# Latent attention: how the rotated queries of head pairs two to four are made and multiplied

## The reference, cut to what matters

```python
q = rms_norm(h @ w_dq) @ w_uq         # 8 heads x (128 plain + 64 rotary columns)
k_rope = rope(h @ w_kr)               # 64 rotary columns, one set for all heads
k_plain, v = split(rms_norm(h @ w_dkv) @ w_ukv)
q = concat(q_plain, rope(q_rope))     # rope: x * cos + swap_halves(x) * (-sin, sin)
s = (q @ concat(k_plain, k_rope).T) / sqrt(192)   # causal, then softmax, then @ v
```

## Time and profile before

| | us |
|---|---|
| median of 3 runs | 1338.31 (1337.6 to 1339.15) |
| the profiled execution's own time | 1336.54 |
| its span in the trace, first to last instruction | 1334.8 |
| PE busy in the span | 1306.4 |
| DVE (VectorE) busy | 754.4 |
| ACT (ScalarE) busy | 524.6 |

### The profile page before, as it was taken

The page is one execution under the profiler, slowest core; times in us unless marked ns, Lnnn a source line. Parts: engine busy times, 40 slices in busy tenths (PEclk is TensorE's granted clock), DMA queues, the critical chain, the costliest instruction groups (busy, mean ns, idle before and its releaser), DMA issues.

```text
span 1334.8 us, 16283 instructions
## 1 busy us (share of the span) xinstructions
PE 1306.4 (98%) x6203; PEld 1080.2 (81%) x6203; DVE 754.4 (57%) x1041; ACT 524.6 (39%) x739; POOL 32.8 (2%) x31
## 2 busy tenths in 40 slices
PE   8999999999999999999999999999999999989997
PEld 7788888888888777788888888888888878878876
DVE  6854544444448675654444544554767578875554
ACT  6443223233334554433223223334233355665334
POOL 0510000000000000000000000000000000010000
PEclk9999999999999999999999999999999999999999
DMA  5343232223242201233222222233543121112211
GB/s 188 95 126 94 94 94 94 79 87 103 90 111 65 57 33 64 79 97 108 94 94 94 94 79 87 88 105 100 158 125 128 32 63 48 48 64 96 95 63 64
DMA packets 120888, 119.43 MB, mean 89 GB/s; under 512 B 13500, under 2 KB 117896, under 8 KB 120584
## 3 DMA queue, kind: packets, MB, share of 16 engines
q1 hardware_dynamic: 120784, 118.76, 28.3%
q10 hardware_dynamic: 56, 0.01, 0.0%
HBM read 114.57 MB, written 4.19 MB: 89 GB/s over the span
## 4 chain that ended last, share of the span: by engine, by line
PE 90%; DVE 5%; ACT 2%; issue 1%; DMA 0%; DVEq 0%; SPq 0%; ACTq 0%
PE psum L1807 27%; PE psum L1809 26%; PE psum L1808 26%; PE psum L1991 1%; PE psum L2014 1%; PE psum L2176 1%; PE psum L2148 1%; PE psum L2162 1%; PE psum L2302 1%; ACT w_hi L647 1%; PE psum L2001 1%; DVE w_lo L1121 1%; PE psum L2256 1%; PE psum L1845 1%; PE psum L1825 0%
## 5 line engine op out<-in xcount | busy, mean ns | idle before, releaser
L1807 PE MATMUL psum<-xg_hi,w_hi 128*128 128x512 f32 x1088 | 432.2, 397 | 1.4 <-DVE emb L1701 0.9
L1809 PE MATMUL psum<-xg_hi,w_lo 128*128 128x512 f32 x1088 | 424.0, 390 | 0.0
L1808 PE MATMUL psum<-xg_lo,w_hi 128*128 128x512 f32 x1088 | 423.8, 389 | 0.0
L1807 PEld LDWEIGHTS psum<-xg_hi,w_hi 128*128 128x128 f32 x1088 | 204.6, 188 | 44.6 <-issue 1.5
L1809 PEld LDWEIGHTS psum<-xg_hi,w_lo 128*128 128x128 f32 x1088 | 204.3, 188 | 43.4
L1808 PEld LDWEIGHTS psum<-xg_lo,w_hi 128*128 128x128 f32 x1088 | 204.6, 188 | 40.4 <-issue 1.2
L1255 DVE TENSOR_TENSOR w_lo<-w_raw,w_hi 128x2048 fp32r<-128x2048 f32 x40 | 91.8, 2295 | 145.6 <-ACT w_hi L740 145.6
L1282 DVE TENSOR_TENSOR w_lo<-w_raw,w_hi 128x2048 fp32r<-128x2048 f32 x32 | 73.4, 2293 | 115.6 <-ACT w_hi L766 115.6
L1807 PE MATMUL psum<-act_hi,w_hi 128*128 128x512 f32 x352 | 137.2, 390 | 0.0
L1808 PE MATMUL psum<-act_lo,w_hi 128*128 128x512 f32 x352 | 137.0, 389 | 0.0
L1809 PE MATMUL psum<-act_hi,w_lo 128*128 128x512 f32 x352 | 136.9, 389 | 0.0
(11 more groups left out here) (355 smaller groups left out, 1614.7 us busy)
## 6 DMA issues: line engine op xcount, KB each, us to landing
w_raw<-in_ffn_w_gate SPq DMA_DIRECT2D x22, 1024.0 KB, 5.1
w_raw<-in_ffn_w_up SPq DMA_DIRECT2D x22, 1024.0 KB, 5.1
w_raw<-in_w_in SPq DMA_DIRECT2D x16, 1024.0 KB, 5.4
w_raw<-in_ffn_w_down SPq DMA_DIRECT2D x16, 768.0 KB, 4.8
w_raw<-in_ffn_w_down SPq DMA_DIRECT2D x16, 640.0 KB, 4.5
w_raw<-in_mla_w_o SPq DMA_DIRECT2D x4, 1024.0 KB, 5.2
w_raw<-in_w_out SPq DMA_DIRECT2D x4, 1024.0 KB, 5.0
w_raw<-in_w_ple_gate SPq DMA_DIRECT2D x4, 1024.0 KB, 4.9
```

The lines of the kernel that those rows point to most:

```text
L1807: pe.matmul(o, wh, xh, start=start, stop=False, skip_group_check=True)
L1808: pe.matmul(o, wh, xl, start=False, stop=False, skip_group_check=True)
L1809: return pe.matmul(o, wl, xh, start=False, stop=stop, skip_group_check=True)
```

## The change

For pairs two to four (pr = 1 to 3) VectorE rotates the queries itself. It multiplies all 128 rows of `u` by cos into `squares[:, 0]` (one instruction), multiplies 32-row quarters by sin into the swapped places of `squares[:, 1]` (four instructions, `rope_swap`, two for each head), and subtracts (one instruction, `rope_sum`). ScalarE rounds each head's 64 rows into half of an fp32r tile (two instructions), and VectorE writes the residue into the other half (two, `rope_lo`). The tiles are free ones of `xg_hi`. The keys' rotated 64 rows are written once as `kr_st`: rounded part twice, on both halves, and residue twice, on both halves (two ScalarE and two VectorE instructions). The rotary score is then two fp32r passes over 128 partitions, the stacked query against the rounded keys and against their residue. Pair one keeps `q_rope` and the fp32 product. `q_rope` has one buffer instead of two.

The order of VectorE for a pair whose `u` is recorded in step s0 (s0 = 4, 12, 20): iteration s0 + 1: cos, first swap, normalise, second swap. Iteration s0 + 2: after the row maximum, `rope_sum`. Iteration s0 + 3: after the residue of `kn0` and after normalising, `rope_lo`. ScalarE's two roundings stand first in its iteration s0 + 3, before the rounding of `kn0`. The bank of `u` is free only after the second swap, and the scores of step s0 + 4 wait for `rope_lo`.

```diff
-        q_rope = sb("q_rope", [P, 2, 2, T], stack=mla_mem)
+        q_rope = sb("q_rope", [P, 2, T], stack=mla_mem)
+        kr_st = sb("kr_st", [P, 2, T], F32R, mla_mem)
...
         def proj_released(x):
+            if x[1] == "u":
+                return sem("rope_turned"), 8 * x[0] + (1 if x[0] else 4)
             return (sem("values_kept"), VALUED.index(x) + 1) if x in VALUED else (sem("proj_ready"), RESIDUED.index(x) + 1)
+        def rope_step(s, later):
+            return [pr for pr in range(1, HEADS // 2) if later < s <= NB * HEADS and (pr, "u") in after_step(*divmod(s - 1 - later, NB))]
+        def rope_tiles(pr, e):
+            x = xg_hi[:, QR + 2 * (pr % 2) + e, :]
+            return (x[64 * e:64 * e + 64, :], x[64 - 64 * e:128 - 64 * e, :], x)
...
@@ ScalarE, for s in range(NB * HEADS + 3): @@
+                    for pr in rope_step(s, 2):
+                        act.wait_ge(sem("rope_turned"), 8 * pr + 2)
+                        act.activation(rope_tiles(pr, 0)[0], squares[0:64, 0, :], ACT.Copy)
+                        act.activation(rope_tiles(pr, 1)[0], squares[64:128, 0, :], ACT.Copy).then_inc(*mark(f"rope_hi{pr}"))
...
+                    if s == 3:
+                        act.activation(kr_st[0:64, 0, :], kr[0:64, :], ACT.Copy)
+                        act.activation(kr_st[64:128, 0, :], kr[0:64, :], ACT.Copy).then_inc(*mark("kr_st"))
...
@@ VectorE @@
+                def rope_swap(pr, e):
+                    ps = proj_result(PROJ_ORDER.index((pr, "u")))
+                    for r0, r1 in ((64 * e, 64 * e + 32), (64 * e + 32, 64 * e)):
+                        dve.tensor_tensor(squares[r0:r0 + 32, 1, :], ps[r1:r1 + 32, :], sin_t[r1:r1 + 32, :], ALU.mult).then_inc(sem("rope_turned"), 1)
+                def rope_sum(pr):
+                    dve.wait_ge(sem("rope_turned"), 8 * pr + 1)
+                    dve.tensor_tensor(squares[:, 0, :], squares[:, 0, :], squares[:, 1, :], ALU.subtract).then_inc(sem("rope_turned"), 1)
+                def rope_lo(pr):
+                    dve.wait_ge(*at(f"rope_hi{pr}"))
+                    for e in range(2):
+                        hi, lo, _ = rope_tiles(pr, e)
+                        dve.tensor_tensor(lo, squares[64 * e:64 * e + 64, 0, :], hi.bitcast(F32), ALU.subtract).then_inc(sem("rope_turned"), 1)
...
                     if what == "u":
...
+                        if pr:
+                            dve.tensor_tensor(squares[:, 0, :], ps[:, :], cos_t[:, :], ALU.mult).then_inc(sem("rope_turned"), 1)
+                            rope_swap(pr, 0)
+                            return
...
@@ VectorE, for s in range(NB * HEADS + 1): @@
                         row_max(s)
+                    for pr in rope_step(s, 1):
+                        rope_sum(pr)
                     if s:
                         for t in after_step(*divmod(s - 1, NB)):
                             proj(*t)
                     if s:
                         normalise(s - 1)
+                    for pr in rope_step(s, 0):
+                        rope_swap(pr, 1)
+                    for pr in rope_step(s, 2):
+                        rope_lo(pr)
+                    if s == 4:
+                        dve.wait_ge(*at("kr_st"))
+                        for r in range(0, P, 64):
+                            low = dve.tensor_tensor(kr_st[r:r + 64, 1, :], kr[0:64, :], kr_st[0:64, 0, :].bitcast(F32), ALU.subtract)
+                        low.then_inc(*mark("kr_lo"))
...
@@ TensorE, scores(s) @@
-                    pe.wait_ge(sem("proj_ready"), proj_count(h // 2, f"kn{h % 2}", f"qn{h % 2}", "u"))
-                    pe.wait_ge(sem("rope_turned"), 3 * (h // 2) + 3)
+                    pe.wait_ge(sem("proj_ready"), proj_count(h // 2, f"kn{h % 2}", f"qn{h % 2}"))
+                    pe.wait_ge(sem("rope_turned"), 8 * (h // 2) + 4)
+                    if s == 2 * NB:
+                        pe.wait_ge(*at("kr_lo"))
...
-                    pe.matmul(o, q_rope[:, h // 2 % 2, hs, q], kr[:, k], start=False, stop=False, skip_group_check=True)
+                    if h < 2:
+                        pe.matmul(o, q_rope[:, hs, q], kr[:, k], start=False, stop=False, skip_group_check=True)
+                    else:
+                        turned_q = rope_tiles(h // 2, hs)[2][:, q]
+                        pe.matmul(o, turned_q, kr_st[:, 0, k], start=False, stop=False, skip_group_check=True)
+                        pe.matmul(o, turned_q, kr_st[:, 1, k], start=False, stop=False, skip_group_check=True)
```

More of the change, by code:

```diff
@@ L62 @@
 MARKS = {
-    "scalar_mark": ("tok_root", "pool_w_hi0", "pool_w_hi1", "pool_w_hi2", "mix_squared", "mix_root", "ffn0_root", "kv_root", "ckv_hi", "rq_root", "attn_root", "ffn1_root", "inner_root",
+    "scalar_mark": ("tok_root", "pool_w_hi0", "pool_w_hi1", "pool_w_hi2", "mix_squared", "mix_root", "ffn0_root", "kv_root", "ckv_hi", "rq_root", "kr_st", "rope_hi1", "rope_hi2", "rope_hi3", "attn_root", "ffn1_root", "inner_root",
                     "gates_ready", "cmp_exp", "fin_root"),
@@ L68 @@
                     "ffn0_rstd", "rkv_ready", "ckv_ready", "kr_ready", "ckv_lo", "rq_ready",
-                    "attn_clear", "attn_rstd", "ffn1_rstd", "inner_ready", "dmask_ready", "kcv_padded", "pe_kept", "gates_kept",
+                    "kr_lo", "attn_clear", "attn_rstd", "ffn1_rstd", "inner_ready", "dmask_ready", "kcv_padded", "pe_kept", "gates_kept",
                     "cmp_shifted", "cmp_probs", "fin_clear", "fin_rstd"),
@@ L226, in program @@
         cos_s, sin_s = probs[:, 0, :], probs[:, 1, :]
-        QN, KN = 0, 2
+        QN, KN, QR = 0, 2, 4
         raw_sem = [sem("weights_loaded0"), sem("weights_loaded1")]
@@ L335, in program @@
         PROJ_ORDER = [(0, what) for what in FIRST_PROJ] + [x for h in range(HEADS) for ii in range(NB) for x in after_step(h, ii)]
-        RESIDUED = [x for x in PROJ_ORDER if x[1][0] != "v"]
+        RESIDUED = [x for x in PROJ_ORDER if x[1][0] not in "uv"]
         VALUED = [x for x in PROJ_ORDER if x[1][0] == "v"]
@@ L1359, in proj @@
                     done = sem("proj_ready")
-                    if idx:
-                        dve.wait_ge(done, RESIDUED.index((pr, what)))
                     if what == "u":
@@ L1364, in proj @@
                         ps = proj_result(idx)
+                        if pr:
+                            dve.tensor_tensor(squares[:, 0, :], ps[:, :], cos_t[:, :], ALU.mult).then_inc(sem("rope_turned"), 1)
+                            rope_swap(pr, 0)
+                            return
                         for e in range(2):
                             r = slice(64 * e, 64 * e + 64)
-                            dve.tensor_tensor(q_rope[0:64, pr % 2, e, :], ps[r, :], cos_t[r, :], ALU.mult).then_inc(sem("rope_turned"), 1)
-                            sine = dve.tensor_tensor(q_rope[64:128, pr % 2, e, :], ps[r, :], sin_t[r, :], ALU.mult)
-                            sine.then_inc(*((done, 1) if e else (sem("rope_turned"), 1)))
+                            dve.tensor_tensor(q_rope[0:64, e, :], ps[r, :], cos_t[r, :], ALU.mult).then_inc(sem("rope_turned"), 1)
+                            dve.tensor_tensor(q_rope[64:128, e, :], ps[r, :], sin_t[r, :], ALU.mult).then_inc(sem("rope_turned"), 1)
                         return
-                    hi = [x for x in RESIDUED if x[1] != "u"].index((pr, what)) + 1
-                    dve.wait_ge(sem("proj_hi"), hi)
+                    n = RESIDUED.index((pr, what))
+                    if n:
+                        dve.wait_ge(done, n)
+                    dve.wait_ge(sem("proj_hi"), n + 1)
                     dve.tensor_tensor(proj_tiles(idx, xg_lo), proj_result(idx), proj_tiles(idx, xg_hi).bitcast(F32), ALU.subtract).then_inc(done, 1)
```

## The result

The changed kernel takes **1350.76 us** (1350.17 to 1351.62, four runs) against 1337.97 before (1337.6 to 1339.15, four runs). The ratio is 1.0099, with a 95% interval of 1.0086 to 1.0111: slower by 12.8 us. Slower was forecast, by 6.1 us and to at most 1348.0; the loss is twice that. The profiled execution took 1350.17 us, its span is 1348.4.

What follows compares the result with a forecast made beforehand. TensorE was taken to bound the kernel, except that VectorE releases steps 8, 16 and 24. Stretches of +3.5, +1.9, +1.9 and -1.2 sum to +6.1 us on 1338.31: 1344.4 us, 8-in-10 range 1340.0 to 1348.0.

Steps and rivals of the forecast that it cites:

- That VectorE's chain releases steps 8, 16 and 24, and each added instruction counts in full: Attention: VectorE runs without a gap from the scores of step s0 + 1; additions lengthen each chain by 3.4 to 3.5 us.
- 0.715 us for every added instruction, whatever its rows: VectorE's eight rotation instructions a pair: cost set by the 512 columns, 0.715 us each, 32-row swaps included.
- ScalarE's roundings, 0.1 to 0.2 us in the chain with an upper end of 0.4: Two roundings before that of kn0, copies 0.49 us apart: VectorE waits about 0.1 us, 0.2 for pair two.
- TensorE's saving, 0.85 a head, counted up to step s0 + 1 only: Rotary passes save 0.85 us a head; 1.5 us counts in each period to steps 16 and 24, 1.2 behind.
- The failed step: the clock: Rival: longer idle before step 8 lowers TensorE's clock, adding 2 to 4 us once, giving 1346.4 to 1348.4; chance 0.11.

Runs made afterwards that it cites:

- VectorE's and ScalarE's part alone: Changed kernel with the two fp32r passes of pairs two to four replaced by one fp32 product of the keys' tile with itself: 1354.02 us, ratio 1.0123.
- the filled run: Changed kernel with extra matmuls in all six TensorE waits (15, 13, 13 before scores of steps 8, 16, 24; 7, 2, 2 before kn0): 1343.86 us.
- the run with three waits filled: Changed kernel with 12 extra matmuls before the scores of each of steps 8, 16 and 24: 1345.39 us, ratio 1.0059.
- the reordered and filled one: Changed kernel with VectorE's and ScalarE's work reordered, plus 8, 4 and 4 extra matmuls before steps 8, 16, 24 and 11 in the later stage: 1335.08 us.
- the reordered one: Changed kernel with u read before the row maximum, residues split around normalising, second head's rounding behind that of kn0: 1337.88 us, ratio 1.0002.
- the one with u read early: Kernel before the change, with VectorE's four products of u moved ahead of the row maximum: 1336.91 us, ratio 0.9995.

## Why the prediction was wrong

- **That VectorE's chain releases steps 8, 16 and 24, and each added instruction counts in full:** right. All three scores wait for the last `rope_lo`, the chains are 11.0 us long, and VectorE's and ScalarE's part alone keeps the whole loss. The reading of the kernel before was a little off: before steps 16 and 24 TensorE's path ended together with VectorE's and was the longer one by 0.13 us.
- **0.715 us for every added instruction, whatever its rows:** right; 32 rows take 0.68 to 0.70.
- **ScalarE's roundings, 0.1 to 0.2 us in the chain with an upper end of 0.4:** wrong, 0.61. The copies start 0.63 apart. The 0.49 was taken from a pair of copies out of PSUM; these read SBUF. From the end of `rope_sum` (475.82) to the residue of kn0 (477.95) it is 2.13 us, where 1.7 was reckoned: 0.3 more for the spacing, the rest for the two hand-overs between the engines. With it the three chains grow by 3.8 to 3.9 us instead of 3.4 to 3.5, 1.2 us in all.
- **TensorE's saving, 0.85 a head, counted up to step s0 + 1 only:** right, 0.82 measured. Behind step 24 it gave 1.4 us (forecast 1.2) once the clock was kept.
- **The failed step: the clock.** The forecast let every wait end at full clock, which puts the lost clock at nothing, and had the fall as a rival only, at 0.11, once, behind step 8 alone. It happened behind all three waits and took 1.3, 2.5 and 1.6 us. The two stretches from step 8 on show where the reasoning broke: the longer waits before steps 16 and 24 (3.28 us) were in the forecast's own sums, as the chain of 3.4 us against no wait before, but the rival's place was only looked for where the wait was longest. The Trainium skill (TensorE: Matmul & The Clock Gate, "Why this matters for your kernels") warns of long gaps between bursts of matmuls. The traces agree for the three waits of 3.28 to 3.96 us, with the clock at 0.50 behind each, so it should have moved the forecast and not only a chance. They do not give a safe length: the clock also fell behind waits of 2.08 to 2.78 us and near one of 1.84.
- **The stage behind attention, costed at nothing:** 1.6 us between the two traces, through the clock again, in code that the change does not touch. Most executions of the kernel before (14 of 21) show a lower granted clock and a time longer by such an amount as well, so between the medians this term may well be nothing.

By size: 6.1 forecast, 0.9 for terms that were mis-sized (7.0 in the filled run's trace) and 5.4 for the clock in attention make 12.4, against 12.8 between the medians. In the spans 1.6 for the clock later comes on top and 0.4 less ahead of attention: 13.6.

## What to carry to other kernels

Where another engine releases the busiest one, a saving on the busiest counts only up to the start of that engine's chain, and everything added behind that start counts in full: look for the place. When a change lengthens waits of TensorE to what lost the clock here (2.1 to 4.0 us), price the lowered clock behind each such wait, not only behind the longest. Executions of one kernel differed by 1.6 us here, so compare those with the same mean granted clock. And before giving up a change like this, move its work: the same instructions in another order took 13 us less.

## What the runs showed of the hardware

- A 512-column fp32r pass starts 0.43 us after the one before at the lower clock and 0.23 at full. Behind waits of 3.3 to 4.0 us the granted clock was 0.50 in a window of 2 us or more and back at 1.00 after 3 to 6 us; one such fall cost 1.3 to 2.5 us. Behind the wait of 1.46 us in the kernel before it stayed at 1.00. No length was found that is safe: in the run with three waits filled it fell at 448.0 us, 1.4 us after a wait of 1.84 had ended, and in the reordered and filled one at 1187.2 us, just behind a wait of 0.58 that followed one of 1.29.
- The same wait, 2.77 us for ScalarE in the same code, had the clock fall in some traces (the changed kernel, the reordered one, the one with u read early) and not in others (the kernel before, the one with all six waits filled). What decides is open; executions of one kernel differ by it. A comparison of two traces can so show 1.6 us in a stage that a change does not touch.
- Matmuls whose results are thrown away made a kernel faster: 5.4 us with 36 of them, 6.9 with 52.
- ScalarE's copies of 512 columns with rounding start 0.63 us apart when they read SBUF, and 0.49 apart in the pairs that read PSUM.
